# Cache transfers moved from ScalarE's queue to GpSimd's, the state's stores to the end of SyncE's, and the slots of the last pass dealt out anew

## The reference, cut to what matters

```
x: 1024 prompt tokens (8 tiles of 128 rows) and 8 sample tokens, D = 1024, fp32
xn = rmsnorm(x);  z = xn @ w_in
x += merged(attention(window 128), pooling, mLSTM; gates of z) @ w_out
xn2 = rmsnorm(x);  q = xn2 @ peer_wq          # 8 heads x 2 x 128
per token and head: top 16 of 128 x 128 pairs of keys -> 16 experts, softmax gates
x += sum over 8 x 16 experts of  gate * gelu(xn2 . u[e]) * v[e]
also returned: the k/v window, the pooling rows and the mLSTM state (C, n, m)
of the prompt, and the same for the 8 samples (k_s, v_s, pool_s, ...)
```

## Time and profile before

| | us |
|---|---|
| median of 3 runs (3653.7 to 3661.3) | 3657.6 |
| the profiled execution | 3654.1 |
| its span, first to last instruction | 3652.3 |
| mean granted TensorE clock | 0.948 |

### The profile page before, as it was taken

The page is one execution under the profiler, slowest core; times in us unless marked ns, Lnnn a source line. Parts: engine busy times, 40 slices in busy tenths (PEclk is TensorE's granted clock), DMA queues, the critical chain, the costliest instruction groups (busy, mean ns, idle before and its releaser), DMA issues. The chain is left out here.

```text
span 3652.3 us, 31475 instructions
## 1 busy us (share of the span) xinstructions
PE 3101.7 (85%) x9934; PEld 1789.2 (49%) x9934; DVE 2292.4 (63%) x5227; ACT 1094.2 (30%) x3297; POOL 1175.9 (32%) x1038
## 2 busy tenths in 40 slices
PE   5699689989997889989988989988998897777777
PEld 3477554445665544446655544443665553222222
DVE  0151477885565768894565779896664577764444
ACT  0120233442222333442213333343221333332222
POOL 0000143332442333443332333442332234444433
PEclk8899899999998989999998999998999899999999
DMA  5234699988999999999999999998998799999998
GB/s 162 87 95 139 253 406 379 416 350 351 415 420 353 418 377 421 420 386 373 420 419 357 407 372 414 387 388 318 417 420 311 296 355 416 421 421 421 421 422 355
DMA packets 204456, 1313.23 MB, mean 360 GB/s; under 512 B 23282, under 2 KB 27434, under 8 KB 71641
## 3 DMA queue, kind: packets, MB, share of 16 engines
q0 software_dynamic: 148608, 1082.20, 72.9%
q1 hardware_dynamic: 49111, 213.07, 15.3%
q10 hardware_dynamic: 6570, 15.94, 1.3%
HBM read 1294.81 MB, written 17.61 MB: 359 GB/s over the span
## 5 line engine op out<-in xcount | busy, mean ns | idle before, releaser
L1974 POOL DMA_INDIRECT arena<-uv,eidx x1032 | 1175.4, 1139 | 2448.2 <-PE ps L894 1785.9
L894 PE MATMUL ps<-arena,dgs 128*128 128x512 f32 x3308 | 1575.9, 618 | 300.3 <-ACT dgs L1227 280.9
L1518 DVE CUSTOM_DVE_ANT_0 arena<-arena,xx 128x1024 f32<-128x1024 f32 x1024 | 1239.9, 1222 | 650.9 <-DMA arena<-uv,eidx 622.3
L894 PEld LDWEIGHTS ps<-arena,dgs 128*128 128x128 f32 x3308 | 626.4, 196 | 1065.5 <-issue 629.6
L1208 ACT ACTIVATE gel<-dots 128x2 f32<-128x2 f32 x516 | 104.4, 202 | 1448.3 <-DVE dots L1518 1447.5
L930 PE MATMUL ps<-wbuf,xT 128*128 128x420 f32 (+1 forms) x1152 | 428.5, 521 | 56.9 <-ACT arena L1284 41.2
L930 PEld LDWEIGHTS ps<-wbuf,xT 128*128 128x128 f32 (+1 forms) x1152 | 204.9, 180 | 280.6 <-issue 261.3
L1105 PE MATMUL ps<-xT,wbuf 128*128 128x256 f32 (+1 forms) x1344 | 318.3, 391 | 12.4 <-DMA wbuf<-w_merge 10.9
L1227 ACT ACTIVATE dgs<-cst,wgt 128x128 f32<-128x128 f32 x827 | 297.7, 396 | 16.7
L1105 PEld LDWEIGHTS ps<-xT,wbuf 128*128 128x128 f32 x1344 | 261.2, 196 | 80.1 <-DMA wbuf<-w_merge 22.2
L1478 DVE SCALAR_TENSOR_TENSOR xx<-arena,wgt,xx 128x1024 f32<-128x1024 f32 x197 | 252.3, 1281 | 66.7 <-ACT wgt L1220 66.6
(11 more groups left out here) (361 smaller groups left out, 1965.3 us busy)
## 6 DMA issues: line engine op xcount, KB each, us to landing
wbuf<-w_merge SPq DMA_DIRECT2D x84, 768.0 KB
wbuf<-w_z SPq DMA_DIRECT2D x64, 840.0 KB
wbuf<-w_q SPq DMA_DIRECT2D x64, 512.0 KB
arena<-uv,eidx POOLq DMA_INDIRECT x1032
wbuf<-w_o SPq DMA_DIRECT2D x32, 512.0 KB
xin<-x_prompt SPq DMA_DIRECT2D x8, 1024.0 KB, 11.1
wbuf<-w_merge SPq DMA_DIRECT2D x12, 512.0 KB
grow<-gains SPq DMA_DIRECT2D x8, 512.0 KB, 8.8
```

The lines of the kernel that those rows point to most:

```text
L894: done = mm(ps[:, half, :], dgs[:, j, :], ring[:, j, row_], start=(q == 0), stop=(q == P - 1), skip_group_check=True)
L1518: v.tensor_tensor_reduce(ring[:, j, 0:D], ring[:, j, 0:D], x, 1.0, 0.0, ALU.mult, ALU.add, dots[:, j:j + 1]).then_inc(s["dotted"], 1)
L1974: g.indirect_dma_start(ring[:, j, :], None, uv, bass.IndirectOffsetOnAxis(ap=experts, axis=0)).then_inc(got[j], 16)
```

## The change

The five transfers of `load_caches` go from ScalarE's queue (in `project` of pass 0) to GpSimd's, right behind its memsets, ahead of the first gather, and signal `caches_in`. `store_last_state` goes from the start of the last `w_o` phase to the end of SyncE's queue, behind the last `w_q` load. `KEPT[3]` is 32, the last pass has weights of its own, and `"o"` lists all eight residues.

```diff
-    output = [(("o", i), 12 / 8) for i in range(NO)]
-    sample = [(("x", i), 3) for i in range(SAMPLE_POINTS)]
+    output = [(("o", i), 14 / 8) for i in range(NO)]
+    last = [(("x", i), 24 / 9) for i in range(SAMPLE_POINTS)]
+    last += [(("m", k, i), 62 / 48) for k in range(3 * KC) for i in range(2)]
+    last += [(("o", i), 20 / 8) for i in range(NO)] + end
...
-                      (p, (sample if p == LAST else []) + merge + output + end + search, own + KEPT[p])]
+                      (p, (last if p == LAST else merge + output + end) + search, own + KEPT[p])]
...
-KEPT = (40, 16, 16, 16)
+KEPT = (40, 16, 16, 32)
...
-ON_VECTOR = {..., "o": (1, 3, 5, 7), "f": (2,)}
+ON_VECTOR = {..., "o": tuple(range(RING)), "f": (2,)}
...
@@ sample_tensor
-            pe.wait_ge(s["k_load"], 16 * 4)
+            pe.wait_ge(s["caches_in"], 16 * 5)
+            pe.wait_ge(s["k_load"], 16 * 2)
...
@@ SyncE
-                weights(w_o, ..., [store_last_state] if p == LAST else [])
+                weights(w_o, ...)
...
+            store_last_state()
             sp.wait_ge(s["sample_y"], 1)
...
-            sp.wait_ge(s["outs"], 16 * 4)
+            sp.wait_ge(s["outs"], 16 * 3)
+            sp.wait_ge(s["caches_in"], 16 * 5)
...
-            sp.wait_ge(s["kscr"], 16 * 4)
+            sp.wait_ge(s["kscr"], 16 * 2)
...
@@ ScalarE, project
-                    if p == 0 and c == 3:
-                        load_caches()
...
@@ GpSimd, after the memsets
+            def load_caches():
+                for rows_, cache, out in ((Ks, cache_k, k_s), (Vs, cache_v, v_s)):
+                    pool.dma_start(rows_[0:W - 1, :, :], cache[:, 1:W, :].rearrange("n k c -> k n c")).then_inc(s["caches_in"], 16)
+                    pool.dma_start(out[:, 0:W - 1, :], cache[:, 1:W, :]).then_inc(s["caches_in"], 16)
+                pool.dma_start(pool_s[:, 0:HIST - 1, :], state_pool[:, 1:HIST, :]).then_inc(s["caches_in"], 16)
+            load_caches()
             fetched = [0]
```

More of the change, by code:

```diff
@@ L98, in share_out @@
             at += w * count / goal
-            last = min(2 * round(at / 2), upto)
-            plan[p][key] = (done, last)
-            done = last
+            to = min(2 * round(at / 2), upto)
+            plan[p][key] = (done, to)
+            done = to
         assert done == upto
     return plan
-KEPT = (40, 16, 16, 16)
+KEPT = (40, 16, 16, 32)
 SOON = (4, 4, 4, 4)
@@ L110 @@
 PLAN = share_out()
-ON_VECTOR = {"z": (3, 7), (LAST, "z"): (1, 3, 5, 7), "b": (1, 5), "m": (1, 4, 6), (LAST, "m"): (1, 3, 5, 7), "o": (1, 3, 5, 7), "f": (2,)}
+ON_VECTOR = {"z": (3, 7), (LAST, "z"): (1, 3, 5, 7), "b": (1, 5), "m": (1, 4, 6), (LAST, "m"): (1, 3, 5, 7), "o": tuple(range(RING)), "f": (2,)}
 def vector_slots():
@@ L147 @@
 state_out_tr state_out_sb consts_in early_out
-outs w_in0 w_in1 kept zs_out zs_in xs_in sample_y state_stored state_c_stored b_n c_load sel_in bsel_in smp_out c_round0 c_round1 c_round2 c_round3 k_load kscr smp_a smp_p smp_v
+outs w_in0 w_in1 kept zs_out zs_in xs_in sample_y state_stored state_c_stored b_n c_load sel_in bsel_in smp_out c_round0 c_round1 c_round2 c_round3 k_load caches_in kscr smp_a smp_p smp_v
 stats_v topk_v""".split()
@@ L847, in _ @@
                         part=lambda i: (2 / 3 if p == 0 and i < EARLY else 0, 1))
-                weights(w_o, (HALF, OC), NO, s["o_mm"], NO * tiles_before(p), tiles, [store_last_state] if p == LAST else [])
+                weights(w_o, (HALF, OC), NO, s["o_mm"], NO * tiles_before(p), tiles)
                 gain(1, 2 * p + 1)
@@ L1249, in norm @@
                       ps[:, b:b + 2, :].rearrange("p a (c n) -> p a c n", c=4)[:, :, :, 0:rows_], ACT.Copy).then_inc(s["xT_ready"], 1)
-            def load_caches():
-                for rows_, cache, out in ((Ks, cache_k, k_s), (Vs, cache_v, v_s)):
-                    act.dma_start(rows_[0:W - 1, :, :], cache[:, 1:W, :].rearrange("n k c -> k n c")).then_inc(s["k_load"], 16)
-                    act.dma_start(out[:, 0:W - 1, :], cache[:, 1:W, :]).then_inc(s["kscr"], 16)
-                act.dma_start(pool_s[:, 0:HIST - 1, :], state_pool[:, 1:HIST, :]).then_inc(s["outs"], 16)
             def spread_bias():
```

## The result

| | before | after |
|---|---|---|
| median of the runs | 3659.5 us (4 runs) | 3615.9 us (4 runs, 3605.8 to 3624.5) |
| profiled execution, its span | 3654.1, 3652.3 us | 3611.6, 3609.7 us |
| first dot product | 434.1 us | 408.9 us |
| last dot product | 3641.7 us | 3599.2 us |

After to before is 0.9881, 95% interval 0.9864 to 0.9898: 44 us faster (37 to 50), where 80 were forecast. The direction was right, the size was half, and the result lies outside the range.

A forecast was written before the change was run, and what follows sets the result against it. DMA bounds the tail at 2.50 us a slot; pass 0 and the last output and find stall on waits. Terms -39 (pass 0), -10 (passes 1, 2), -4 (pass 3), -27 (tail) sum to -80: 3577 us, range 3555 to 3605.

The forecast's parts named there:

- the 3 us for the caches beside `w_z`: Pass 0: the moved cache transfers, 2.26 MB, would delay the stream of `w_z` by 3 us, most falling where DMA is idle.
- the bounds of 0 to 28: Pass 0: cost of the moved caches, from 0 (DMA has room) to 28 us (12.6 us bias wait scaled to 2.26 MB).
- Rival (b): Pass 0: caches beside the first weights cost 28 us instead of 3, whole kernel 3602 us; chance 0.1.
- Nothing waits on GpSimd's queue before the first gather.: Pass 0: GpSimd awaits its first gather for 419 us, which hides any issue time, even 79.9 us.
- GpSimd's 13.4 us wait for TensorE goes, of which I count 7: Output of passes 1 and 2: this wait goes; 7 us counted, as DMA worked for others in part of it.
- It fits: Output and norm, passes 1 and 2: VectorE's 14 dots and rows plus residual take 38 of 58 us.
- The 3 us I gave the find for two slots fewer: Find of passes 1 and 2: two slots fewer save 2 to 5 us, taken as 3.
- Rival (c): Last pass is full: find pays 2.5 us for each of 8 slots, output stays at 79 us; 3596 us, chance 0.12.
- the latency of 9.3 us: Tail, slots 880 and 896: a gather issued into an empty ring is worked on 9.3 us later; used to price the gates.
- Rival (a): Tail: the gates don't bite, 10 of their 12 us stay away, whole kernel 3567 us; chance 0.12.
- Stores in the tail (1 us): Tail: state stores, 0.26 MB and 512 small packets, fall in DMA-bound time and cost 1 us (0.6 to 3).
- rival (d): Output: VectorE holds up gathers, issues of 3.7 us cost 58 us over 48 slots; 3635 us, chance 0.03.

The follow-up runs named there:

- the floor: Changed kernel with neither cache loads nor copies to the outputs, the two SBUF tensors set to zero: 0.9805 to the kernel before, first dot product at 385.6 us.

## Why the prediction missed

- **Pass 0 (-39, measured -25).** The step that failed is the 3 us for the caches beside `w_z`. I priced them by bytes and idle DMA time. The measured cost is the distance to the floor, 408.9 to 385.6: 23 us, and 28 in the slowest of the kernels with the same start; also the 5.4 us that I had estimated from the bytes fall short of it. The cost lies at the upper end of the bounds of 0 to 28 that I had from the spreading of the bias; I took the other end, and the price hung on the form of the load. Rival (b) was the case, at nearly its price. The waits themselves, 26.1 us in six pieces, are inside the bound of 30 named for them, and 14.9 of it had stood there before; but the matmuls that restart slowly behind each wait, which the forecast counted as a gain of 1 us, became a loss of 7 (the projection's matmuls take 435.3 us on the page after, 428.5 before, nearly all of it in pass 0).
- **"Nothing waits on GpSimd's queue before the first gather."** Right as it stood, and the run with the loads beside the find shows how much hung on it: the first dot product comes 32 us later as soon as a gather stands behind them.
- **Passes 1 and 2 (-10, measured +10).** The step "GpSimd's 13.4 us wait for TensorE goes, of which I count 7" failed. The wait for TensorE went and a wait for VectorE took its place, and TensorE's 11 us of additions had stood in its waits for `w_o`. "It fits" was true of VectorE's sum, 43.7 in 61.5 us, and not enough: the ring place comes free one VectorE row after the dot. The 3 us I gave the find for two slots fewer did not come either; it stayed at 182. The two passes are not of one kind: with 12 slots again pass 1 stays 3 us longer than before and pass 2 does not.
- **Pass 3 up to the merge's end (-5, measured -6).** Right in size, by luck: the merge, which was to give 5, gave 2.6, and the samples' part, whose slots did not change, gave 6.2 against 3.3 lost ahead of it. That part took 94.9 to 96.8 us in most kernels of either plan; 98.0 before and 91.8 after are its two ends.
- **Last output and norm (72 forecast, 74.8 measured).** Right: the stores' 13 us are worth what the rows said there (13.1 alone), and the output could carry 20 slots.
- **Find of pass 3 (177 forecast, 185.4 measured).** The step that failed is that the find pays for its slots alone. The stores leave in its last 39 us and cost it some 4 us. The other 12 us are 1.5 us for each of the eight slots, where I had taken 1; by the run with eight slots fewer it is 0.9, and the traces do not settle which. Rival (c) had the find at +20 and the output at +0; the measured +16 and -4 lie between it and my sum.
- **Tail (-27, measured -37).** The 2.50 us a slot held. The gates were charged 12 us and cost 5: the step that failed is the latency of 9.3 us, taken from the kernel's first gather, where a gather in the tail takes 5.7 to 6.1. Rival (a), by which 10 of the 12 us stay away, was the nearer: 7 did, though not because the gates came early, as GpSimd does wait for them.
- **Stores in the tail (1 us).** Wrong in place: they leave in the find, where they cost some 4 us, and the tail is as long with them moved (589.6) as without (589.5).
- **The rest (+3.6)** is pass 2's branches at a lower granted clock, which changes from trace to trace; what lowers it there is not shown.
- **The range** took in (b) or (c), not both with the outputs the other way round: the misses of 14, 20 and 11 us all had the same sign, against 10 in the tail.

What stays open: why the outputs' matmuls ran at a lower clock, whether as a cause of their length or as a consequence of TensorE's waits; how much of the 1.57 us a gather takes to issue belongs to VectorE's rows; and what a slot costs in the last find. Adding on VectorE in some other pattern than 8, 4 or 1 in eight was not tried, nor the split loads on ScalarE's queue.

## What to carry to other kernels

Price a transfer that moves beside others by the form in which it was seen, not by its bytes: look at its issue time, its landing time (with a semaphore of its own) and the small packets, and if its partitions are a number like 127, try it split, here as 112 and 15, before moving it. A transfer put last in a queue leaves when that queue is through, not when the kernel ends: the stores meant for the tail went out in the find. A wait that is taken away shows who was hidden by it. When work is moved from one engine to another inside a stretch, ask who frees the ring place then, not whether the sum of busy time fits. A latency belongs to its state: the kernel's first gather is no measure for one in the middle of the stream.

## What was unexpected of the hardware

- A load of 127 partitions (508 KB) from GpSimd's queue took 6.9 us to issue and 47.1 to land, and the queue's next load came 42 to 53 us after it, wherever it stood. As 112 and 15 partitions it took 1.70 us to issue, and both loads with all copies had landed 16 us after the first was issued.
- The landing times of transfers that share a semaphore can be mixed up: the profile has 25.1 us for that load beside a copy, and 47.1 without. The copy has 42.3, so it seems to be held up by the load.
- A stream of 840 KB weight loads on another queue lost 23 us to two such loads of half a megabyte each and the copies beside them (21 to the loads alone), while the DMA engines were busy in half of the time. The window of the changed kernel, columns as in the earlier trace rows:

```profile
0.00:130.00 130.00, 92.18 (x235) 48.51 (x236) 11.25 (x26) 16.47 (x27) 15.70 (x11) 0.91 0.50 157
```

- With all additions of the output on VectorE, a gather's issue rose from 1.28 to 1.57 us in the mean of pass 1's output, and from 0.94 to 1.93 in the median. The Trainium skill, "SBUF — State Buffer", section "SBUF: two separate sides", has a lock between VectorE with two SBUF inputs and GpSimd reading SBUF; the trace agrees in direction, but parts it from nothing else that VectorE does there, and at 0.3 us a gather it is far from the price of rival (d).
- The wait behind the 512 single elements of `n_p` was 13.2 us with idle DMA beside it and 24.1 us with gathers that filled it.
